# A convolution mixer rearranged: two projections first, convolution taps spread over all blocks, a modulation row group moved behind the mixer

## The reference, cut to what matters

```python
def odd_mixer(u, conf_dw, conf_dw_b, conf_ln_g, conf_ln_b, sc_dw):
    a, gate, sb, scc, sx = jnp.split(u, [...], axis=-1)          # five parts of 512
    conf = a * jax.nn.sigmoid(gate)
    conf = depthwise_conv(conf, conf_dw) + conf_dw_b             # 31 taps
    conf = jax.nn.silu(group_layer_norm(conf, conf_ln_g, conf_ln_b, CONF_GROUPS))
    sc = sb * depthwise_conv(scc * sx, sc_dw)                    # 3 taps
    return jnp.concatenate([conf, sc], axis=-1)

mix = odd_mixer(h @ b_w_in[j], ...) @ b_w_out[j]
x = x + g1 * mix
```

## Time and profile before

| | |
|---|---|
| device time, median of 3 | 1167.72 us (1165.39 to 1170.78) |
| the profiled execution | 1173.12 us, span 1171.3 us |
| PE busy | 1107.9 us (95%) |
| DVE / ACT / POOL busy | 778.2 (66%) / 556.6 (48%) / 124.1 us (11%) |
| mean granted TensorE clock | 0.964 of full |
| chain that ended last | PE 78%, DVE 8%, DMA 5%, POOL 3%, ACT 3% |
| mixer of layer 1 | about 424 to 541 us of the span |

### The profile page before, as it was taken

The page is one execution under the profiler, slowest core; times in us unless marked ns, Lnnn a source line. Parts: engine busy times, 40 slices in busy tenths (PEclk is TensorE's granted clock), DMA queues, the critical chain, the costliest instruction groups (busy, mean ns, idle before and its releaser), DMA issues.

```text
span 1171.3 us, 21316 instructions
## 1 busy us (share of the span) xinstructions
PE 1107.9 (95%) x8488; PEld 1013.8 (87%) x8488; DVE 778.2 (66%) x1296; ACT 556.6 (48%) x947; POOL 124.1 (11%) x139
## 2 busy tenths in 40 slices
PE   7888998999999999779999999999899998999998
PEld 2867857899999988768999999988776698999998
DVE  0756775677888757857667776756535857666665
ACT  3533265544344367746434444522326755454542
POOL 1101002000000018811000000300002410000000
PEclk9888999999999989889999999999999998999999
DMA  9953144388898844424878776445431223555550
GB/s 364 407 204 111 54 128 164 132 333 339 331 350 330 332 143 169 180 90 146 303 269 287 263 274 217 146 143 181 140 126 39 77 92 133 190 198 182 176 180 36
DMA packets 68310, 232.98 MB, mean 199 GB/s; under 512 B 12112, under 2 KB 12400, under 8 KB 67856
## 3 DMA queue, kind: packets, MB, share of 16 engines
q1 hardware_dynamic: 62208, 227.27, 54.2%
q0 software_dynamic: 5888, 3.73, 1.2%
q10 hardware_dynamic: 144, 1.05, 0.3%
HBM read 230.91 MB, written 1.05 MB: 198 GB/s over the span
## 4 chain that ended last, share of the span: by engine, by line
PE 78%; DVE 8%; DMA 5%; POOL 3%; ACT 3%; issue 2%; DVEq 0%; SPq 0%; POOLq 0%; ACTq 0%
PE bank L1462 23%; PE bank L1463 22%; PE bank L1464 22%; POOL vals L549 3%; DMA bias<-rpb 2%; DVE w_lo L942 2%; DMA a_raw<-ada 2%; PE bank L1598 2%; DVE big L1018 1%; PE bank L1485 1%; PE bank L1514 1%; ACT w_hi L576 1%; PE bank L1506 1%; PE bank L1936 1%; DVE h_lo L1026 1%
## 5 line engine op out<-in xcount | busy, mean ns | idle before, releaser
L1462 PE MATMUL bank<-h_hi,w_hi 128*128 128x256 f32 (+1 forms) x1664 | 495.1, 298 | 23.9 <-DVE h_lo L1026 11.5
L1463 PE MATMUL bank<-h_lo,w_hi 128*128 128x256 f32 (+1 forms) x1664 | 486.8, 293 | 0.0
L1464 PE MATMUL bank<-h_hi,w_lo 128*128 128x256 f32 (+1 forms) x1664 | 486.2, 292 | 0.0
L942 DVE TENSOR_TENSOR w_lo<-w_raw,w_hi 128x1024 fp32r<-128x1024 f32 x281 | 341.6, 1238 | 98.1 <-ACT w_hi L576 96.9
L1462 PEld LDWEIGHTS bank<-h_hi,w_hi 128*128 128x128 f32 x1664 | 325.6, 196 | 40.7 <-issue 14.2
L1463 PEld LDWEIGHTS bank<-h_lo,w_hi 128*128 128x128 f32 x1664 | 326.3, 196 | 3.4 <-issue 0.2
L1464 PEld LDWEIGHTS bank<-h_hi,w_lo 128*128 128x128 f32 x1664 | 325.9, 196 | 3.6
L576 ACT CAST w_hi<-w_raw 128x1024 fp32r<-128x1024 f32 x281 | 287.2, 1045 | 58.6 <-PE bank L1464 58.1
L1462 PE MATMUL bank<-g_hi,w_hi 128*128 128x256 f32 x528 | 148.7, 282 | 0.9 <-DVE g_lo L1144 0.9
L1463 PE MATMUL bank<-g_lo,w_hi 128*128 128x256 f32 x528 | 148.3, 281 | 0.0
L1464 PE MATMUL bank<-g_hi,w_lo 128*128 128x256 f32 x528 | 148.2, 281 | 0.0
(11 more groups left out here) (150 smaller groups left out, 1104.0 us busy)
## 6 DMA issues: line engine op xcount, KB each, us to landing
w_raw<-weights SPq DMA_DIRECT2D x281, 512.0 KB, 4.6
a_raw<-ada SPq DMA_DIRECT2D x144, 512.0 KB, 5.3
bias<-rpb POOLq DMA_DIRECT2D x16, 224.0 KB, 7.3
xT<-xt SPq DMA_DIRECT2D x1, 1024.0 KB, 9.5
big<-ctx SPq DMA_DIRECT2D x1, 1024.0 KB, 8.3
big<-ctx ACTq DMA_DIRECT2D x1, 1024.0 KB, 7.3
out_t<-xT SPq DMA_DIRECT2D x2, 512.0 KB, 2.6
con<-consts SPq DMA_DIRECT2D x1, 928.0 KB, 10.1
```

The costliest lines, as they stand in the source:

```text
L942: nc.vector.tensor_tensor(w_lo[:, s, :], w_raw[:, s, :], w_hi[:, s, :].bitcast(fp), SUB)\
L1462: nc.tensor.matmul(out, a_hi, b_hi, start=start, stop=False)
L1463: nc.tensor.matmul(out, a_hi, b_lo, start=False, stop=False)
L1464: return nc.tensor.matmul(out, a_lo, b_hi, start=False, stop=stop)
```

## The change

The input projection starts with two blocks multiplied together, input tile by input tile, where it was four. Taps on ACT are three for each block j from 3 to 19 (five at j = 2) with the rest behind the loop, where they were five for each up to j = 14; taps on DVE are four for each block up to j = 18, where they were five up to j = 15. The sums of the group norm's half 0 stand one block earlier or later: `conf_sum(0)` behind block 12 (it was 13), `conf_squares(0)` behind 14 (15), `conf_spread(0)` behind 17 (16). `conf_sum(1)` moves from behind the input projection into the output projection, ahead of input tile 6, and `conf_squares(1)` moves from ahead of tile 6 to ahead of tile 0. Row group 26 (eight products of `a_raw`) moves out of the input projection: half of it ahead of `conf_spread(1)`, half ahead of input tile 2, its copy on ACT behind the mixer's casts, its columns ahead of block 6 of the output projection. SP issues the four `ada` blocks of group 27 ahead of the load of block `W_OUT1 + 5`, where it was `W_OUT1`. On DVE the casts' remainders of half 0 stand ahead of `conf_normed(1)`.

```diff
-    at[W_IN1 + 20] = 104
+    at[W_OUT1 + 5] = 104
@@ ACT
-                if j == 7:
-                    ada_copy(26)
-                if j == 12:
+                if j == 13:
                     centred_square(0)
-                if j == 13:
+                if j == 15:
                     root(("conf", 0), P)
                 if j >= 2:
-                    tap_products(min(5, CONF_K * (1 + (j > 6)) - made[0]))
+                    tap_products(min(5 if j == 2 else 3, len(POOL_TAPS) - made[0]))
+            tap_products(len(POOL_TAPS) - made[0])
             centred_square(1)
...
+            ada_copy(26)
             project_out(W_OUT1, 4)
@@ DVE
+                    if layer == 1 and j == 6:
+                        ada_take(26)
...
-                if 3 <= j < 16:
-                    conv_taps(max(0, min(5 * (j - 2), CONF_K * (1 + (j >= 7))) - taps_done[0]))
+                if 3 <= j < 19:
+                    conv_taps(max(0, min(4 * (j - 2), CONF_K * (1 + (j >= 7))) - taps_done[0]))
-                if j == 11:
+                if j == 12:
                     centre(0)
-                if j == 13:
+                if j == 16:
                     invert(("conf", 0))
-                if j == 14:
+                if j == 18:
                     conf_normed(0)
-                if j == 19:
-                    centre(1)
             short_low(CG - 1)
+            centre(1)
             invert(("conf", 1))
-            conf_normed(1)
-            for g in range(CG):
+            for half in range(2):
+                if half:
+                    conf_normed(1)
+                for g in (2 * half, 2 * half + 1):
@@ PE
-                between = {6: lambda: conf_squares(1), 0: lambda: conf_spread(1)} if layer == 1 else {}
+                def first_half_sums():
+                    conf_squares(1)
+                    ada_rows(26, range(4))
+                    conf_spread(1)
+                between = {6: lambda: conf_sum(1), 0: first_half_sums,
+                           2: lambda: ada_rows(26, range(4, KT))} if layer == 1 else {}
...
+                    if layer == 1 and j == 6:
+                        ada_columns(26)
...
-            project_four([("in1", j) for j in range(4)], W_IN1, xs, range(KT), lambda k: (hlo_ready, 3 * KT + k + 1))
+            project_four([("in1", j) for j in range(2)], W_IN1, xs, range(KT), lambda k: (hlo_ready, 3 * KT + k + 1))
-                if j == 6:
-                    ada_rows(26)
-                if j == 8:
-                    ada_columns(26)
-                if j == 13:
+                if j == 12:
                     conf_sum(0)
-                if j == 15:
+                if j == 14:
                     conf_squares(0)
-                if j == 16:
+                if j == 17:
                     conf_spread(0)
-            conf_sum(1)
             project_out(1, W_OUT1)
```

More of the change, by code:

```diff
@@ L374, in place_ffn @@
                 last_taken[6] = last_taken[7] = (conv_done, 2)
+                place_rows(26)
             for j in range(KT):
@@ L393, in program @@
         place_rows(25)
-        place_rows(26)
         for j in range(N_IN1):
@@ L1401, in _ @@
                         short_low(g - 1)
-                if 3 <= j < 16:
-                    conv_taps(max(0, min(5 * (j - 2), CONF_K * (1 + (j >= 7))) - taps_done[0]))
-                if j == 1:
+                if 3 <= j < 19:
+                    conv_taps(max(0, min(4 * (j - 2), CONF_K * (1 + (j >= 7))) - taps_done[0]))
+                if j == 2:
                     ada_take(25)
-                if j == 8:
-                    ada_take(26)
-                if j == 11:
+                if j == 12:
                     centre(0)
-                if j == 13:
+                if j == 16:
                     invert(("conf", 0))
-                if j == 14:
+                if j == 18:
                     conf_normed(0)
-                if j == 15:
-                    conv_taps(len(tap_list) - taps_done[0])
-                if j == 19:
-                    centre(1)
             short_low(CG - 1)
+            centre(1)
             invert(("conf", 1))
-            conf_normed(1)
-            for g in range(CG):
-                dve.wait_ge(o_hi, 12 + g + 1)
-                nc.vector.tensor_tensor(h_lo[:, g, 0:T], cacc[:, g, :], h_hi[:, g, 0:T].bitcast(fp), SUB)\
-                    .then_inc(o_lo, 1)
+            for half in range(2):
+                if half:
+                    conf_normed(1)
+                for g in (2 * half, 2 * half + 1):
+                    dve.wait_ge(o_hi, 12 + g + 1)
+                    nc.vector.tensor_tensor(h_lo[:, g, 0:T], cacc[:, g, :], h_hi[:, g, 0:T].bitcast(fp), SUB)\
+                        .then_inc(o_lo, 1)
             project_out(1, W_OUT1)
@@ L1884, in conf_spread @@
                 spread(("inv", "conf", half), [column(c0 + t) for t in range(4)])
-            for j in range(3, N_IN1):
-                if j == 3:
+            for j in range(2, N_IN1):
+                project(("in1", j), W_IN1 + j, xs, T)
+                if j == 2:
                     ada_columns(25)
-                if j > 3:
-                    project(("in1", j), W_IN1 + j, xs, T)
                 if j == 4:
                     cond_spread(1)
-                if j == 6:
-                    ada_rows(26)
-                if j == 8:
-                    ada_columns(26)
-                if j == 13:
+                if j == 12:
                     conf_sum(0)
-                if j == 15:
+                if j == 14:
                     conf_squares(0)
-                if j == 16:
+                if j == 17:
                     conf_spread(0)
-            conf_sum(1)
             project_out(1, W_OUT1)
```

## The result

The changed kernel takes 1175.03 us, median of 8 runs (1171.87 to 1177.63), the kernel before 1167.96 us in the same comparison (8 runs, 1165.39 to 1171.68). The ratio is 1.0058, 95% interval 1.0038 to 1.0077: the change costs 7.1 us (4.4 to 9.0). The forecast was 1171.7 us and +4.0; the time lies in the range and the direction is that of the sum. But the case that I held likeliest (0.40) ended at +5.8 us, the 0.5% that a measurement can tell, and the measured +7.1 lies in the band above it, which had 0.30.

What follows compares the result with a forecast made beforehand. PE was 95% busy, with POOL's 60 additions the mixer stage's backbone. Starting 3.7 us earlier, POOL would end 4.5 us later; with the tail and held load the stage ends at 544.7, not 540.7: +4.0, 1171.7 us, range 1160.5 to 1177.5.

Steps and rivals of the forecast that it cites:

- the case that I held likeliest: Whole execution: the forecast's own case, a change of -1 to +5.8 us, chance 0.40.
- part 1: Start of the input projection: two projections first let POOL's first addition begin at 434.7, 3.7 us earlier.
- part 3: Stop at `conf_sum(0)`: PE waits 4.5 us for POOL's thirtieth addition, then runs at half clock; POOL gets a 2.2 us gap.
- part 4: Blocks 16 to 19: rounds of 4.2 us leave POOL idle; it ends at 507.4, 4.5 us later, delaying `conf_sum(1)`.
- part 5: Behind `conf_sum(1)`: tile 0 ready at 517.9, PE idle 2.0 us, tiles and row products done at 521.7.
- part 6: Block 4 of the output projection: load held behind group 27 makes PE wait 5.4 us; stage ends at 544.7, +4.0 us.
- Parts 2 and 3: Three taps per block: PE runs ahead of POOL (3.4 us per block against 2.9), then waits 4.5 us at `conf_sum(0)`.
- the sign that I gave: POOL's timeline: idle gaps summing to 7 to 9 us, last addition ending at 505 to 509.
- the strong form of (a): POOL fed in time, quick load and no clock drop at block 4: -6.5 us, 1161.2 us; chance 0.14.
- (a): Rival, blocks 16 to 19: POOL is fed in time, ends near 500.9; -2.5 to -6.5 us; chances 0.12 weaker, 0.14 strong.
- (b): Rival, weight block 5's load takes 8.2 us: PE waits 8.6 us, +7.2, 1174.9; 0.30 together with longer starvation of POOL.
- (c): Rival, the change does what it says: POOL never holds PE, -15 us, 1153 us; chance 0.04.

Runs made afterwards that it cites:

- the experiment that does it alone: Kernel before with only the two projections first, the other 18 one by one, taps, sums and row group as before: 1164.93 us, ratio 0.9988.
- The experiment that feeds POOL in blocks 16 to 19: Changed kernel with ACT's three tap products of blocks 16 to 19 ahead of its wait for DVE's factor: 1169.99 us, ratio 1.0022.
- the sum at tile 7: Changed kernel with row group back in the input projection, taps first in blocks 16 to 19, eight products at block 2, `conf_sum(1)` ahead of tile 7: 1159.39 us.
- the fastest kernel: Changed kernel with row group back in the input projection, taps first in blocks 16 to 19, eight products at block 2, `conf_sum(1)` ahead of tile 6: 1157.40 us.
- the load freed: Changed kernel with group 27's `ada` loads issued ahead of `W_OUT1 + 8` instead of `W_OUT1 + 5`: 1168.60 us, ratio 1.0008.

## Why the prediction was right, and where it was not

Set both from the first product of the input projection (424.23 in the forecast, 420.59 in after's trace):

| mark | forecast | measured |
|---|---|---|
| first addition of POOL (part 1) | 10.5 | 10.5 |
| `conf_sum(0)` starts (part 3) | 44.8 | 45.2 |
| POOL's first addition of block 16 (part 4) | 62.8 | 63.9 |
| `conf_sum(1)` starts (part 4) | 83.2 | 84.2 |
| tile 0 starts (part 5) | 93.7 | 94.1 |
| block 4 of the output projection starts (part 6) | 105.8 | 107.1 |
| end of the stage | 120.5 | 121.4 |

**Part 1** held: 3.7 us forecast, 3.7 in after, 3.5 by the experiment that does it alone.

**Parts 2 and 3** held in kind. PE waited 4.63 us at `conf_sum(0)` (forecast 4.5), and ran the sum at half clock. Mis-sized was what comes behind it: I let POOL lose 2.2 and 1.9 us until block 16, and it lost 0.98, 2.96 and 2.34, 2.2 us more in all; its additions until there took 1.1 us less than I had them. The net, 1.1 us by which block 16's additions are late, is about the whole error of the sum (0.9 us).

**Part 4**, the step on which I said most depends, came out nearly as forecast: additions start at 484.44, 488.62, 492.80 and 496.97, 4.18 us apart (forecast 4.2), and last 7.71 us behind (7.9). What it says of POOL inside the round is wrong: three additions take 3.51 us there, not 2.6, since one of them is stretched beside a split, so POOL idles 0.67 us in each round and not 1.6. The time of the round did not need this. But the sign that I gave, gaps of 7 to 9 us in all, was then met in part by luck: I had 2.2 and 1.9 us until block 16 and 4.8 in the rounds, and 6.3 and 2.0 came. Making the taps ahead of ACT's wait in these blocks gave back 4.0 us.

**Part 5** gave the right time from `conf_sum(1)` on (37.2 us for parts 5 and 6; forecast 37.3), but one sentence of it stops short: that the row products and the columns "cost PE the same 1.85 + 0.85 us here as there". They cost PE the same 2.7 us in both places, but the stage next to nothing in the old one, where PE's stops take them up. The sum didn't feel this, since it was made along the new order; the reading of the change did. I had filed the move as a held load and nothing more ("the one new wait that nothing hides"); it is a held load and 3.6 us, ACT's copy among them. Part 5 also has no word on PE's 4.29 us stop at 496.41, ahead of tiles 4 and 5. PE had to wait for POOL behind it all the same (3.29 us; forecast some 4), so a shorter one would not have brought the sum forward.

**Part 6** held: 5.86 us of wait (forecast 5.4). The load took 5.3 us from its issue at 519.66 to the cast at 524.97 (5.0), and its issue came 0.6 us later behind tile 0 than I had it. The two `ada` blocks right ahead were there as forecast. My bounds for the load rest on a misread row, though: the 5.8 us in the earlier trace rows are of a weight load issued at 433.26, just ahead of its four `ada` blocks (433.63); the two issued behind four such blocks took 7.1 and 6.0 us. Of the load, the Trainium skill ("DMA: Bandwidth & Descriptors", Anatomy of one DMA) would make an estimate of 3.2 us, and of the wait 2.1 us less; the trace doesn't agree, and the measurement decides. Loads with nothing just ahead took 3.3 to 3.5 us here. The Trainium skill's "SBUF — State Buffer", Who interferes with whom, again fits: in after, too, POOL's addition takes 0.74 us at the median and up to 1.84, as in the earlier trace rows beside a split.

**Small slips in the sums.** 487.0 + 3 x 4.2 is 499.6, not 499.5; the lower end of the range, 1160.5, is 0.7 below the strong form of (a) that it is said to be (1161.2). Neither changes the reading.

**The size.** The sum gave +4.0, the stage shows +5.0, the medians +7.1. The stage's number is inside the interval (4.4 to 9.0), and so it is in each of the other nine comparisons. But in nine of the ten the medians lie 1.0 to 2.5 us above what the stages say (the tenth, the fastest kernel, lies 0.8 below). These are not ten separate witnesses: there are four sets of runs of the kernel before, one of them shared by four kernels and one by another four. One explanation would be that the one profiled execution of before had a longer stage than it usually has. The other traces speak against it: the kernel with the row group moved alone, the same up to `conf_sum(1)` but for that group, needs 79.7 us to there (before: 80.0), and the kernel with two projections first, the same behind it, needs the same 36.4. So the 2 us between stage and medians stay open. They are what took the result over the 0.5%.

**What the parts add up to.** The held load is +5.1, the place with its copy +3.6, the taps' order in blocks 16 to 19 +4.0, the two projections first -3.4: together +9.3, where the stage shows +5.0. If the parts simply add, the other 4.3 us are gained by what no run takes alone (the sums' new places, the taps' spreading); which of it, is not shown.

**The rivals.** (a) would have needed POOL's gaps under 2 us; they were 8.3. The experiment that feeds POOL in blocks 16 to 19 halves them (4.1 us are left) and gives 4.0 us of stage; the rest of (a) was not run in the changed kernel. (b), a load of over 6.8 us, did not occur. (c) did not either: even without a gap, POOL's 60 additions took 64.4 us, and every kernel here except the one with the sum at tile 7 begins `conf_sum(1)` within 1.4 us of POOL's last addition.

## What to carry to other kernels

Find the engine on whose count a join waits and follow it first: here the stage is POOL's end plus a tail, and an edit ahead of the join pays by what it moves POOL, as long as PE isn't late at the join itself (the sum at tile 7: POOL 2.0 us earlier, the stage 0.3). Filler work belongs ahead of a join that PE must wait for anyway, and its cost is seen only in the pair "here or there", not in the work itself. When work on a slot of a ring moves later, the loads that reuse the slot move with it, and everything queued behind them on the issuing engine. A stretch with DMA share 0 tells where to look, but is no cost by itself: with the load freed, three more loads went out ahead of it and `conf_sum(1)` started no earlier to speak of (84.2 and 83.9). What was paid is the one load that came too late for block 5.

## What the runs showed of the hardware

- The clock behind a wait of PE. Behind waits of 0.40, 0.63, 0.81 and 1.66 us the sum of the taps took 1.10 us, behind 2.99, 3.29, 4.63 and 5.22 us it took 2.04 to 2.05, the same two instructions at half speed. The granted clock says the same. Below are the windows of two sums, after's `conf_sum(1)` and the fastest kernel's, with the clock as the third number from the end: 0.50 (1.2 GHz) and 1.00 (2.4 GHz). This is no sharp line: behind a stop of 3.06 us the first product of the output projection took 0.35 us in one kernel and 0.55 in another, behind 3.09 us the first of a spread 0.38 or 0.58, and behind 2.02 us the first product of tile 0 0.39 or 0.58. So a wait can cost more than its own length: with the load freed, 4.4 us less wait made 4.8 us less behind `conf_sum(1)`.

```profile
504.78:506.90 2.12, 2.12 (x4) 1.08 (x5) 0.04 (x1) 0.00 (x0) 0.00 (x0) 0.50 0.00 0
```
```profile
501.00:502.10 1.10, 1.10 (x4) 0.62 (x5) 0.00 (x0) 0.00 (x0) 0.00 (x0) 1.00 0.00 0
```

- A 512 KB load with two `ada` blocks of the same size issued 0.5 and 0.9 us ahead of it, and two more 7.4 us and longer ahead, which had landed, was there 5.3 us after its issue; with nothing just ahead such loads took 3.3 to 3.5 us.
